# Output projection of a fused transformer layer: three more seven-product k pairs, and the last PE transposes of one mixer moved to DMA

## The reference, cut to what matters

```python
D_MODEL = 4096; SEQ = 256          # all float32
# h  = rmsnorm(x) @ w_in           four token mixers: b (DSA), c (NSA), d (dilated), a (stick-breaking)
# m  = sum over the mixers of sigmoid(gate) * (mixer output @ its projection)
# x1 = x + m @ w_out                                   ("output projection")
# y  = x1 + PEER(rmsnorm(x1))                          w_q, keys, top-k, u, v
def masked_softmax(s, mask):
    e, _, den = softmax_stats(s, mask)
    return e / jnp.maximum(den, jnp.finfo(jnp.float32).tiny)
```

## Time and profile before

| | |
|---|---|
| median of three executions | 1890.02 us (1889.78 to 1890.89) |
| the profiled execution | 1890.36 us |
| its span in the trace | 1888.5 us |
| granted TensorE clock, mean | 1.0 of full speed |
| PE busy | 1883.6 us (100% of the span), 8837 matmuls and transposes |
| DVE busy | 1506.1 us (80%) |
| ACT busy | 987.8 us (52%) |
| POOL busy | 72.1 us (4%) |
| DMA | 423.97 MB, mean 224 GB/s |

### The profile page before, as it was taken

One profiled execution on the slowest core, in us unless ns is written; L12 is line 12 of the kernel. 1 busy time (PEld: TensorE's weight loads), 2 busy tenths in 40 slices (PEclk: granted clock), 3 DMA queues, 4 the chain that ended last, 5 costly groups with the idle time before them and its releaser, 6 DMA issues.

```text
span 1888.5 us, 25682 instructions
## 1 busy us (share of the span) xinstructions
PE 1883.6 (100%) x8837; PEld 1556.2 (82%) x8837; DVE 1506.1 (80%) x2198; ACT 987.8 (52%) x1207; POOL 72.1 (4%) x109
## 2 busy tenths in 40 slices
PE   9999999999999999999999999999999999999999
PEld 8888878878888888888888888888888888888887
DVE  6578875685566889989887655899989978999897
ACT  6654644445466655546554464444444455555553
POOL 0010020211100000000000000000000000000000
PEclk9999999999999999999999999999999999999999
DMA  9976668767675569867778776667766678666664
GB/s 317 355 227 169 181 199 239 201 170 243 203 233 177 181 194 288 279 231 232 221 249 277 236 228 218 232 205 222 219 203 200 201 216 285 223 216 225 207 221 156
DMA packets 202386, 423.97 MB, mean 224 GB/s; under 512 B 46752, under 2 KB 125216, under 8 KB 201504
## 3 DMA queue, kind: packets, MB, share of 16 engines
q1 hardware_dynamic: 174048, 369.35, 63.1%
q0 software_dynamic: 7248, 27.92, 4.2%
q10 hardware_dynamic: 20976, 25.19, 4.1%
HBM read 395.79 MB, written 26.61 MB: 224 GB/s over the span
## 4 chain that ended last, share of the span: by engine, by line
PE 99%; DMA 0%; SPq 0%; ACT 0%; DVE 0%; issue 0%
PE acc L709 25%; PE acc L712 25%; PE acc L716 25%; PE acc L757 3%; PE acc L759 3%; PE acc L763 3%; PE acc L1195 2%; PE side L1074 1%; PE side L1073 1%; PE side L1075 1%; PE acc L1201 1%; PE acc L1114 1%; PE acc L1120 1%; PE acc L1115 1%; PE side L884 1%; PE side L1001 1%
## 5 line engine op out<-in xcount | busy, mean ns | idle before, releaser
L1664 DVE TENSOR_TENSOR w_lo<-w_raw,w_hi 128x1024 fp32r<-128x1024 f32 (+1 forms) x643 | 776.5, 1212 | 331.1 <-ACT w_hi L1242 324.5
L1242 ACT ACTIVATE w_hi<-w_raw 128x1024 fp32r<-128x1024 f32 (+1 forms) x643 | 674.0, 1052 | 696.5 <-PE acc L716 537.3
L709 PE MATMUL acc<-w_hi,xt_hi 128*128 128x512 f32 x1288 | 350.3, 394 | 0.0
L712 PE MATMUL acc<-w_hi,xt_lo 128*128 128x512 f32 x1288 | 344.5, 389 | 0.0
L716 PE MATMUL acc<-w_lo,xt_hi 128*128 128x512 f32 x1288 | 344.4, 389 | 0.0
L709 PEld LDWEIGHTS acc<-w_hi,xt_hi 128*128 128x128 f32 x1288 | 239.9, 188 | 53.1 <-issue 4.9
L712 PEld LDWEIGHTS acc<-w_hi,xt_lo 128*128 128x128 f32 x1288 | 241.7, 188 | 50.7
L716 PEld LDWEIGHTS acc<-w_lo,xt_hi 128*128 128x128 f32 x1288 | 241.7, 188 | 50.5
L709 PE MATMUL acc<-w_hi,x_hi 128*128 128x512 f32 x640 | 173.5, 393 | 0.0
L712 PE MATMUL acc<-w_hi,x_lo 128*128 128x512 f32 x640 | 171.3, 389 | 0.0
L716 PE MATMUL acc<-w_lo,x_hi 128*128 128x512 f32 x640 | 171.2, 389 | 0.0
(11 more groups left out here) (387 smaller groups left out, 2209.2 us busy)
## 6 DMA issues: line engine op xcount, KB each, us to landing
w_raw<-in_stream SPq DMA_DIRECT2D x504, 512.0 KB, 4.2
w_raw<-in_w_in SPq DMA_DIRECT2D x16, 496.0 KB, 4.8
w_raw<-in_w_in SPq DMA_DIRECT2D x16, 480.0 KB, 5.3
w_raw<-in_w_in SPq DMA_DIRECT2D x16, 464.0 KB, 3.9
w_raw<-in_w_in SPq DMA_DIRECT2D x16, 448.0 KB, 3.8
w_raw<-in_w_in SPq DMA_DIRECT2D x16, 432.0 KB, 4.1
w_raw<-in_w_in SPq DMA_DIRECT2D x16, 416.0 KB, 4.5
w_raw<-in_w_in SPq DMA_DIRECT2D x16, 400.0 KB, 3.8
```

The lines of the kernel that those rows point to most:

```text
L709: pe.matmul(o[h], lhs(k0 + j, h)[0], wh[j], start=first and j == 0, stop=False)
L712: pe.matmul(o[h], lhs(k0 + j, h)[1], wh[j], start=False, stop=False)
L1242: nc.scalar.activation(w_hi[:, slot, 0:width], w_raw[:, slot, 0:width], ACT.Copy).then_inc(hi_ready, 1)
L1664: nc.vector.tensor_tensor(w_lo[:, slot, 0:width], w_raw[:, slot, 0:width], w_hi[:, slot, 0:width].bitcast(F32), ALU.subtract).then_inc(lo_ ...
```

## The change

- **Fast k pairs.** Pair 0 has (8, 10, 12) instead of (8, 10), pairs 1 and 2 have (0, 2, ..., 12) instead of (0, 2, ..., 10): 17 instead of 14. Group 1 of the activations' sums holds three k pairs instead of two, so its tensors are half as large again (1536, 384 and 768 elements a partition in place of 1024, 256 and 512). With kp 12 in the set the pure sums of pairs 0 and 1 are added at kp 14 and 15, where they stood at 13 and 14.
- **The third pair.** Its pure sums go to four tiles of their own, `third_sums` (`third_pure`: 5 operations at kp 14 and 15, where `add_pure` had 9), and to the rows after the banks (`add_third`, 4 operations at slot 362). `end_of_pair(2)` waits for x's loads 4 and 5 instead of `pure_free`. x's load 6 no longer waits for the third `pure_free`. `copy_rows` of groups 4 and 5 wait for the third `pure_free`, and `h_hi` waits for all fast k pairs from group 1 on (before: from group 2).
- **ROW_END.** Group 1: 316 to 342; 2: 342 to 350; 3: 350 to 356; 4: 360 to 364; 5: 368 to 370.
- **Heads of b** go over DRAM: transposes at slot 60, copy at slot 65. Three of its four turns on PE go (4, 4 and 2 transposes), and (61, ..., (5, 6)) stays.
- **Probabilities of passes 4 and 7** go over DRAM: 2 x 4 transposes on PE and 2 copies on ACT go. All passes weigh the values at slot +12 (before +10, or +7 for those two); `out_hi` and `out_lo` follow at +15 and +16. Passes 1, 8 and 9 begin one or two slots earlier.

```diff
-OUT_PAIRS = (Pair(0, CH_OUT, FAST[4:], 0), Pair(1, CH_OUT + 2 * CPG, FAST, 2), Pair(2, CH_OUT + 4 * CPG, FAST, 8))
-OUT_T = 14
+OUT_PAIRS = (Pair(0, CH_OUT, FAST_LAST[4:], 0), Pair(1, CH_OUT + 2 * CPG, FAST_LAST, 3),
+             Pair(2, CH_OUT + 4 * CPG, FAST_LAST, 10))
+OUT_T = 17
...
-         (61, 2, "b", (5, 6)), (62, 3, "b", (0, 1)), (64, 2, "b", (2, 3)), (65, 3, "b", (4,))]
-BLOCKED = {"c": (106, 113, 6, 1), "d": (148, 156, 8, 2), "a": (182, 191, 8, 1)}
+         (61, 2, "b", (5, 6))]
+BLOCKED = {"b": (60, 65, 5, 1), "c": (106, 113, 6, 1), "d": (148, 156, 8, 2), "a": (182, 191, 8, 1)}
...
-PASS_AT = (75, 82, 115, 121, 127, 133, 139, 145, 159, 165)
+PASS_AT = (75, 81, 115, 121, 127, 133, 139, 145, 157, 163)
...
-    ROW_END = {n: CH_OUT + {0: 2 * CPG, 1: 2 * CPG + 20, 2: 4 * CPG + 14, 3: 4 * CPG + 22, 4: 6 * CPG, 5: 6 * CPG + 8}.get(n, (n + 1) * CPG)
+    ROW_END = {n: CH_OUT + {0: 2 * CPG, 1: 4 * CPG + 14, 2: 4 * CPG + 22, 3: 6 * CPG - 4, 4: 6 * CPG + 4, 5: 6 * CPG + 10}.get(n, (n + 1) * CPG)
...
-                    if s == at_slot + 5 and i not in BY_BLOCK:
-                        turn_probs(i)
-                    if s == at_slot + (10 if i in BY_BLOCK else 7):
+                    if s == at_slot + 12:
                         weigh_values(i)
...
-                if n >= 2:
+                if n >= 1:
                     act.wait_ge(t_used, OUT_T)
...
             def copy_rows(n):
+                if n in (4, 5):
+                    act.wait_ge(pure_free, 3)
...
-                k0, nq = 16 * g, 4 - 2 * g
+                k0, nq = 16 * g, 4 - g
...
+            def third_pure(step):
+                p1, p5, p6, p7 = (side[:, i, :] for i in range(4))
+                a11, a21, a12, a22 = (t[:] for t in third_sums)
+                if step == 0:
+                    dve.wait_ge(t_used, OUT_T)
+                    then(nc.vector.tensor_copy(a11, p1))
+                elif step == 1:
+                    then(nc.vector.tensor_tensor(a21, p6, a11, ALU.add))
+                elif step == 2:
+                    then(nc.vector.tensor_tensor(a12, p5, a21, ALU.add))
+                    then(nc.vector.tensor_tensor(a21, p7, a21, ALU.add))
+                else:
+                    then(nc.vector.tensor_tensor(a22, p5, a21, ALU.add))
+            def add_third(pair):
+                evacuated(dve, GN_OUT + 5)
+                for n, (i, h) in enumerate(((0, 0), (0, 1), (1, 0), (1, 1))):
+                    c = block_rows_of(pair, i, h)
+                    e = nc.vector.tensor_tensor(c, third_sums[n][:], c, ALU.add)
+                e.then_inc(pure_free, 1)
...
             def end_of_pair(pair, i):
-                dve.wait_ge(pure_free, pair.order + 1)
+                if pair.order == 2:
+                    dve.wait_ge(x_loaded[4 + i], 16)
+                else:
+                    dve.wait_ge(pure_free, pair.order + 1)
...
-                late = pair.fast[-1] == 12 or pair.order == 2
+                late = pair.fast[-1] == 12
...
                 if n == 4:
                     pool.wait_ge(t_used, OUT_T)
-                if n == 6:
-                    pool.wait_ge(pure_free, 3)
```

More of the change, by code:

```diff
@@ L231, in last_part @@
     return br != "c" or part == 0
[L234 to L239, removed]
 def build(nc, io):
@@ L317, in build @@
     head_blk, head_in, head_d = {}, {}, {}
-    for b, to in (("c", [MG0 + 8 * KB]), ("d", [PJ0 + i * row + in_cols(9).start * 4 for i in range(2)]),
+    for b, to in (("b", [cursor[0]]), ("c", [MG0 + 8 * KB]), ("d", [PJ0 + i * row + in_cols(9).start * 4 for i in range(2)]),
                   ("a", [XT0 + 40 * KB])):
@@ L415, in build @@
     out_s_raw = at("out_s_raw", [P, 4, 4, P], F32, MG0 + 24 * KB)
[L416 to L417 removed]
+    out_s_hi = [at(f"out_s_hi{g}", [P, 4, 4 - g, P], F32R, PJ0 + (30 - 18 * g) * KB) for g in range(2)]
+    out_s_lo = [at(f"out_s_lo{g}", [P, 4, 4 - g, P], F32R, PJ0 + (38 - 20 * g) * KB) for g in range(2)]
     out_t_raw = at("out_t_raw", [P, 2, 2, 512], F32, MG0 + 8 * KB)
     out_t_hi = at("out_t_hi", [P, 2, 2, 512], F32R, MG0 + 24 * KB)
[L420 to L422 removed]
+    out_t_lo = at("out_t_lo", [P, 2, 2, 512], F32R, PJ0 + 4 * KB)
+    out_sums = [[at(f"out_sums{n}{i}", [P, 512], F32, MG0 + (8 + 2 * i) * KB) for i in range(2)] for n in range(2)]
+    third_sums = [at(f"third_sums{i}", [P, 512], F32, PJ0 + (40 + 2 * i) * KB) for i in range(4)]
     t_tiles = {True: (out_t_raw, out_t_hi, out_t_lo), False: (t_raw, t_hi, t_lo)}
@@ L886, in scores @@
                 mm.then_inc(scores_ready, 1)
[L888 to L897, removed]
             def weigh_values(i):
                 br, h, part = PASSES[i]
[L901 to L904, removed]
+                pe.wait_ge(probs_moved, 16 * (i + 1))
                 if first_part(br, part):
@@ L909, in weigh_values @@
                 if (br, part) == ("c", 0):
-                    mm = pe.matmul(side[:, 3, :], v_cmp[:], probs_t[0:NCMP, 0, :, :], start=False, stop=True)
+                    mm = pe.matmul(side[:, 3, :], v_cmp[:],
+                                   probs_in[i][0:NCMP, :, 0].rearrange("p a r t -> p r a t"), start=False, stop=True)
                 elif br == "d":
@@ L1344, in exponentials @@
                 e.then_inc(exp_ready, 1)
-            def copy_probs(i):
-                act.wait_ge(probs_turned, turned_before(i) + 1)
-                act.wait_ge(pv_done, i)
-                nc.scalar.activation(flat(probs_t[0:NCMP, 0, :, :]), side[0:NCMP, 0, :], ACT.Copy)\
-                    .then_inc(probs_copied, 1)
             def out_hi(i):
@@ L1547, in between @@
                         exponentials(i)
-                    if s == at_slot + 8 and i not in BY_BLOCK:
-                        copy_probs(i)
-                    if s == at_slot + (13 if i in BY_BLOCK else 10) and last_part(PASSES[i][0], PASSES[i][2]):
+                    if s == at_slot + 15 and last_part(PASSES[i][0], PASSES[i][2]):
                         out_hi(i)
@@ L1885, in block_probs @@
                     dve.wait_ge(head_copied, head_parts("c"))
+                if (br, part) == ("c", 0):
+                    nc.vector.transpose(probs_blk[i][:, 0, 0], q[:, :, 0:32]).then_inc(probs_blocked, 1)
+                    return
                 for s in range(h + 1):
@@ L2443, in pair_tasks @@
             def pair_tasks(pair, kp, i, after):
-                late = pair.fast[-1] == 12 or pair.order == 2
+                late = pair.fast[-1] == 12
                 if late:
                     for step, at in enumerate(((14, 1), (14, 1), (15, 0), (15, 1))):
-                        if at == (kp, i):
+                        if at == (kp, i) and pair.order == 2:
+                            third_pure(step)
+                        elif at == (kp, i):
                             add_pure(pair, step)
@@ L2481, in _ @@
                         end_of_pair(ended, 1)
+                        if ended.order == 2:
+                            add_third(ended)
                 if pair:
```

75 lines of the change are left out of this document (37 added, 38 removed).

## The result

The changed kernel takes **1896.37 us** (median of seven, 1895.70 to 1898.35), the kernel before 1889.98 (median of seven, 1889.35 to 1890.89): ratio 1.0035, interval 1.0026 to 1.0044. It is slower by 6.4 us, where 1889.8 was forecast with a range up to 1892.4. The profiled execution is one of 1896.37 us, with a span of 1894.6 against 1888.5.

What follows compares the result with a forecast made beforehand. PE's instruction list was taken to bound the kernel: 1890.36 - 4.2 saved + 0.45 + 0.55 + 3.0 of stalls = 1890.1 for a profiled-like execution, median 0.34 lower: 1889.8 us. The 8-in-10 range was 1886.3 to 1892.4.

Steps and rivals of the forecast that it cites:

- PE bound, what is saved: PE's instruction list sets the time; three more fast k pairs save 2.04 us, fewer transposes 2.2, together 4.2.
- The attention region at no cost: Slots 60 to 179: waits behind DMA trips for b's heads and the values cost PE 0, range 0 to 1 us.
- Rival E: b's heads come late at slot 65 through slow transposing DMA: some 48 us, time 1938; chance 0.02.
- stall 2: Slot 280, kp 8: DVE's low sums of the activations come late for PE, 0.55 us.
- stall 1: Slot 277: group 1's larger activation sums delay ACT's high part of chunk 277, so PE waits 0.45 us.
- Stall 3: Slot 360: PE waits 3.0 us for DVE's bank-freeing adds, as ACT, held by kp 12, starts DVE late.
- From there DVE has no gap: From 995.96, low part of chunk 355, DVE works without idling until the bank's adds end at 1013.29.
- The bound of 3.5: Upper end of the 0 to 3.5 us range for PE's wait at slot 360.
- rival C: Four x loads together near 994.1 slow the weight loads fourfold; the slot 360 wait becomes 8.1 us, time 1894.9; chance 0.1.
- A: No new wait of PE anywhere, the cover holds: 1885.8 us; chance 0.09.
- B: Only the waits at slots 277 and 280 occur; DVE reaches the bank's adds in time: 1886.8 us; chance 0.19.
- D: Pair 1's adds delay PE 0.3 to 1.5 us at slots 312 to 320, besides the three stalls: 1890.1 to 1891.3; chance 0.06.

Runs made afterwards that it cites:

- x later: Changed kernel, but x's loads 6 and 7 leave only once slots 364 and 368 are used, so two x loads leave together, not four: 1891.48 us.
- the transpose later: Changed kernel with ROW_END of group 3 at 358 instead of 356, so its DVE transpose follows the adds that free the bank: 1893.74 us.
- the output projection alone: Kernel before with only the output projection's change (three more fast k pairs, third pair's own sums, new row slots), heads and probabilities as before: 1898.07 us.
- the `row_t` load later: Changed kernel, but ACT issues group 2's load of row_t at slot 361 instead of 359, with that group's high halves one slot later: 1892.16 us.
- one move that kept the wait under 2 us: Changed kernel with the high halves of group 1's rows one slot later on ACT, at slots 355 and 356: 1890.22 us.

## Why the prediction was wrong

- **PE bound, what is saved.** Right. The transposes were worth 2.24 us (forecast 2.2), the k pairs 0.68 each, less 0.4 us at the starts of pairs 1 and 2 that the prediction didn't have.
- **The attention region at no cost.** Right. ACT took b's heads at 165.39 us without a wait, earlier than the 167 reckoned from c's trip. The Trainium skill's rule for transposes ("VectorE: DVE Perf Modes", section "Rules for kernel authors") speaks for TensorE; this stretch, where TensorE is the only engine without time to spare, won 2.24 us by leaving it. Rival E fell: no run shows a part of its 48 us.
- **Stalls 1 and 2.** The places and the releasers were right in this profile, the sum was 1.57 against 1.0: 0.35 at slots 274 and 275, where DVE's low part of chunk 274 did not "just hold", 0.72 at slot 277 and 0.52 at kp 8. That these come near the forecast is in part luck, as nine profiles have the same output projection code in these slots: stall 2 is in all of them, with 0.3 to 1.9 us, but stall 1 is in three (0.7 us), and in the six others slot 277 loses 0.12 at most. ACT's waits for `mix_t` near 761 and 770 us, which the prediction left out, differ between the profiles: 3.15 us for the first in the changed kernel, where ACT ran into the saturated stretch late, 0.57 with x later, where there is no stall 1. But with the transpose later ACT waited 0.93 and 3.23 and lost 0.12, so the link is argued and not shown.
- **Stall 3, the step that failed.** "From there DVE has no gap" was wrong: DVE stood 1.87 and 0.69 us for ACT, and PE waited 5.7 us instead of 3.0. The list itself was right to 0.1 us (17.2 us against 17.3 with x later, wait 2.94 against 3.0, in one execution). The gap came from ACT, in front of the `row_t` load, behind stores that took 6.7 us instead of 2.9. The load, its slot and its wait for `row_stored` stood in ACT's order, and I counted only `h_hi` and the high parts there. The bound of 3.5 had nothing in it for such a gap. I had costed x's burst in rival C as a delay of weight loads, with 1894.9 for it; the cause was that one, the victim that PE felt was another. The weights' loads were late too: chunk 359's took 7.8 us and chunk 361's 5.6, just short of the 8.5 and 5.9 from which C would have decided. With the output projection alone they took 8.9 and 6.3, over both, and the chain still runs through the stores, the last of which took 8.4. What the weights' loads were worth is 0.7 us, in the run with the `row_t` load later.
- **The clock, the term that was missing.** 2.99 us. I priced PE's wait at its length, as if PE went on at full speed behind it. With it the time passes every rival's but E's: forecast 1889.8, + 2.9 for the wait, + 3.0 for the clock, + 0.6 for stalls 1 and 2, gives 1896.3 against 1896.37. That it comes out so close is luck: the 0.4 us lost at the starts of pairs 1 and 2 and the 0.5 us won at the program's start are not in it and nearly cancel.
- **Rivals.** A and B fell, and so did D: slots 312 to 320 lost under 0.1 us. C had the side right and the mechanism half.

## What to carry to other kernels

A wait of the bounding engine costs more than its length where its clock falls behind it; so a margin of zero is worth less than it seems, and one move that kept the wait under 2 us won back more than the wait's own difference. When a step is moved, go through every instruction ahead of it on the waiting engine, the issues of DMAs with their waits too: an issue that waits for other DMAs to land ties compute to queue traffic. Transfers that were spread by chance (here four x loads by two different waits) are best kept spread when the waits are simplified, above all near transfers that an engine stands and waits for.

## What was not expected of the hardware

- The granted clock behind an idle PE: 1.8, 2.9 and 3.6 us of idle time left it at full in the profiled executions, 3.9, 4.2, 5.7 and 6.2 brought it to half, for 1.5 to 3.0 us of loss. The border isn't known more closely than that: seven of the nine other executions of the version with 2.9 us and all nine of that with 3.6 recorded a mean clock under 1.0, and how long PE waited in them isn't known.
- With x's four loads beside them, the 128 KB stores took 6.7 us instead of 3.5 with two (x later), and the 512 KB weight loads 6.3 instead of 4.7. The Trainium skill, "DMA: Bandwidth & Descriptors", section "Queues, rings and completion order", has the engines take turns between queues by packet; that both kinds slow down fits this, but it gives no size, and why the stores slowed more wasn't tried here.
